# Encoder layer on one core: thirteen more wait instructions in each gate tile of TensorE's program

## The chip, the cores and the metric

The kernel runs on one core of a Trainium2 chip. The metric is the device time of one execution in microseconds; lower is better.

## What is computed

One layer of a bidirectional encoder on a sequence of 256 tokens with 2048 channels, in float32. Cut to what matters:

```python
xn = _rmsnorm(x, norm_pre_w[l])
h = xn @ w_in[l]                       # 256 x 2048 times 2048 x 13312
na_q, na_k, na_v, na_z, hg_q, hg_ff, hg_fb, hg_i, hg_z, gate_pre = jnp.split(h, splits, axis=-1)
o_a = neighbourhood_attention(na_q, na_k, na_v, na_rel_bias[l]) * silu(na_z)      # 16 heads of 64
o_b = rmsnorm(hgrn2_bidirectional(hg_q, hg_ff, hg_fb, hg_i, lb)) * silu(hg_z)     # 8 heads of 128
g = jax.nn.sigmoid(gate_pre + b_gate[l]); g_a, g_b = jnp.split(g, 2, axis=-1)     # gate_pre: 256 x 4096
y = g_a * (o_a @ w_branch[l, :NA_WIDTH]) + g_b * (o_b @ w_branch[l, NA_WIDTH:])
x = x + _rmsnorm(y @ w_out[l], norm_post_w[l])
```

## The kernel before, in words

It is written instruction by instruction: each engine has its own program, and semaphores join them. Nearly all of TensorE's work is matrix products in split precision. SyncE loads a weight tile of 1 MB into one of four `raw` buffers; ScalarE rounds each half of it into `w_hi` (L522, counted by `hi_ready`); VectorE makes the remainder `w_lo` (L762, counted by `lo_ready`); TensorE multiplies hi with hi, hi with lo and lo with hi, and tells with `half_used` that a half is free.

TensorE's program is straight code, with every loop written out when it is built. Its parts are:

- 16 early tiles (L1303) for the values of both branches;
- 8 groups of 10 tiles, one group per head pair and head (`group`, L1430). Slots 0, 1, 3, 4, 5, 7 and 9 are channel tiles (`project`, L1213): 16 products of 512 columns with `w_hi` (L1222), then 16 of 256 columns with `w_lo` (L1229). Slots 2, 6 and 8 are gate tiles (`gate_tile`, L1254, through `token_tile`, L1233): 16 products of 512 columns with `w_hi`, then 8 with `w_lo`, all on L1237;
- a tail of 8 gate tiles;
- 16 tiles of the branch projection (`token_tile` again, from `branch_tile`), and 16 tiles of the output projection (L1497 to L1499).

Between the `w_hi` and the `w_lo` products of a tile, `visits` (L1415) puts in TensorE's small work for attention and recurrence. Most of it stands in slot 3, after the 16 long products of that channel tile:

```python
if s == 3:
    if g > 0:
        heads_out(g - 1)       # 8 products, L1348
        near_session(g - 1)    # 64 products, L1370 and L1362
    if g < NG:
        both_scores(g)         # 16 products, L1335
    if g > 0:
        far_scores(g - 1)      # 2 products, L1390
```

These 90 products are in float32, each done by the engine as two matmuls, so 180 matmuls with their 180 weight loads. They are called the burst here. The burst of group g belongs to `visits(g, 3)`; the tail has one too, without `both_scores`. Slots 5 or 6 and 7 or 8 hold 4 and 2 small products more.

The first product of a channel tile waits for `hi_ready` and for `tile_out`, so one of these two stands alone; the first product of a gate tile waits for `hi_ready` only, but for the first gate tile of a block of four.

Of the kernel before, what the change touches and what calls it, by code (L numbers as in the profile page):

```python
# [47 lines left out]
IN_SLOTS = 10  # L48
I_SLOTS = (30, 31)
TAIL = 8  # L50
PRE_BLOCKS = 4
N_PRE = 4 * PRE_BLOCKS
M_IN = NG * IN_SLOTS + TAIL
N_IN = N_PRE + M_IN
# [50 lines left out]
def encoder_layer(nc, x_head, x_turned, x_rows, vectors, w_in, band_bias, b_gate, w_branch, w_out, norm_post_w, out):  # L105
# [4 lines left out]
    with ExitStack() as ctx:  # L110
        def sb(name, shape, dt=F32):
            return ctx.enter_context(nc.sbuf_tensor(name, shape, dt))

        def sem(name):
            return ctx.enter_context(nc.semaphore(name))

        act_hl = sb("act_hl", [P, KT, 2 * T], F32R)
# [3 lines left out]
        w_hi = sb("w_hi", [P, HALVES, 1024], F32R)  # L122
# [56 lines left out]
        def gate_sums(b):  # L179
            return bank[0:2] if b == GATE_BLOCKS - 1 else bank[2:4]  # L180
# [30 lines left out]
        hi_ready = sem("hi_ready")  # L211
# [46 lines left out]
        def wait(engine, semaphore, value):  # L258

            if isinstance(value, int) and value <= 0:  # L260
                return
            engine.wait_ge(semaphore, value)
# [13 lines left out]
        def gate_tile_of(g, s):  # L276

            return divmod(g * len(GATE_SLOTS) + (s if g == NG else GATE_SLOTS.index(s)), 4)
# [6 lines left out]
        def raw_count(n4, r):  # L285

            return n4 * 16 + (16 if r > 1 else 0)

        def place(g, s):

            n = g * IN_SLOTS + (N_PRE + s)
            return n, n % RAW, raw_count(n // RAW, n % RAW)
# [61 lines left out]
        def _(sp):  # L354
# [12 lines left out]
            def time_order(g):  # L367

                if g == 0:
                    sp.wait_ge(block_taken, 2 * PRE_BLOCKS)  # L370
                wait(sp, hg_out, g - 1)
# [7 lines left out]
            def load_gates(g, s):  # L379

                n, r, _ = place(g, s)
                b, part_k = gate_tile_of(g, s)
                col = GATE_TILE * P + 512 * b
                load(r, w_in_v[:, 4 * part_k:4 * part_k + 4, col:col + 512], n)

            def group(g):
                for s in range(IN_SLOTS):
                    if s == 1:
                        load_bias(g)
                    if s == 4:  # L390
                        time_order(g)
                    n, r, _ = place(g, s)
                    if s in GATE_SLOTS:
                        load_gates(g, s)
                    else:
                        col = g + COL_TILE[s]
                        load(r, w_in_v[:, :, col * P:col * P + P], n)
# [34 lines left out]
            for g in range(NG):  # L432
                group(g)
            for t in range(TAIL):
                load_gates(NG, t)
# [78 lines left out]
        def _(act):  # L514
# [10 lines left out]
            def split_tile(n, r, landed):  # L525
                split_hi(n, r, landed, 0)
                split_hi(n, r, landed, 1)
# [83 lines left out]
            def group(g, first):  # L611
                for s in range(IN_SLOTS):
                    split_tile(*place(g, s + 1))
                    if first and s == 0:
                        take_block(PRE_BLOCKS - 1)
                    if not first:
                        previous(g, s)
                    attention(g, s)
                    if s in CHANNEL_SLOTS:
                        take_part(place(g, s)[0], turn(g, s) % 2)  # L620
# [22 lines left out]
            def take_block(c):  # L643

                act.wait_ge(half_used, 8 * (c + 1))
                if c == 0:
                    act.wait_ge(rstd_ready, 1)
                for t in range(2):
                    src = bank[4 + 2 * (c % 2) + t].rearrange("p (g c) -> p g c", g=4)
                    nc.scalar.activation(token_tiles(c // 2, c % 2, t), src, ACT.Copy,  # L650
                                         scale=rstd[:, t:t + 1]).then_inc(block_taken, 1)
# [33 lines left out]
            for g in range(NG):  # L685
                group(g, g == 0)
            for t in range(TAIL):
                split_tile(*place(NG, t + 1))
# [65 lines left out]
        def _(dve):  # L754
# [10 lines left out]
            def split_tile(n, r):  # L765
                split_lo(n, r, 0)
                split_lo(n, r, 1)
# [241 lines left out]
            def group(g, first):  # L1009
                for s in range(IN_SLOTS):  # L1010
                    split_tile(*place(g, s + 1)[0:2])
                    if not first:
                        previous(g, s)
                    attention(g, s, first)
                    if s == 6 and not first:
                        mean_square(g - 1)
                    if s in GATE_SLOTS:
                        take_gates(g, s)
                    else:
                        take_tile(g, s, tile_dst[s])  # L1020
# [76 lines left out]
            for g in range(NG):  # L1097
                group(g, g == 0)
            for t in range(TAIL):
                split_tile(*place(NG, t + 1)[0:2])  # L1100
# [111 lines left out]
        def _(pe):  # L1212
# [17 lines left out]
                                               stop=(k == KT - 1), skip_group_check=True)  # L1230
                    ins.then_inc(half_used, 1)

            def token_tile(n, operand, sums, part_k, begin, end, between):  # L1233

                def product(t, h, kk, lo, weights, start=False, stop=False):
                    k, w = 4 * part_k + 2 * h + kk, slice(kk * 512, (kk + 1) * 512)
                    return nc.tensor.matmul(sums[t][:, :], operand[:, k, lo * T + t * P:lo * T + (t + 1) * P],  # L1237
                                            weights[:, (2 * n + h) % HALVES, w], start=start, stop=stop)

                for h in range(2):  # L1240
                    pe.wait_ge(hi_ready, n * 2 + h + 1)
                    for t in range(2):
                        for kk in range(2):
                            product(t, h, kk, 0, w_hi, start=(begin and h == 0 and kk == 0))
                            product(t, h, kk, 1, w_hi)
                between()
                for h in range(2):
                    pe.wait_ge(lo_ready, n * 2 + h + 1)
                    for t in range(2):
                        for kk in range(2):  # L1250
                            ins = product(t, h, kk, 0, w_lo, stop=(end and h == 1 and kk == 1))
                    ins.then_inc(half_used, 1)

            def gate_tile(g, s, between):  # L1254

                b, part_k = gate_tile_of(g, s)
                if part_k == 0 and b == GATE_BLOCKS - 1:
                    pe.wait_ge(tile_out, NG * len(CHANNEL_SLOTS))
                elif part_k == 0:
                    wait(pe, gate_out, 2 * b)  # L1260
                token_tile(place(g, s)[0], act_hl, gate_sums(b), part_k, part_k == 0, part_k == 3, between)

            def warm(count):
                for _ in range(count):
# [58 lines left out]
            def both_scores(g):  # L1323
# [3 lines left out]
                if g == 0:  # L1327
                    pe.wait_ge(band_clear, 3)
                    pe.wait_ge(block_taken, 2 * PRE_BLOCKS)
                for u in range(2):  # L1330
# [8 lines left out]
            def heads_out(g):  # L1339
                pe.wait_ge(prob_ready, g + 1)  # L1340
                v_now = big[:, 2 * g, :]
                if g == 0:
                    pe.wait_ge(block_taken, 2 * PRE_BLOCKS)
                wait(pe, oa_ready, g)
# [70 lines left out]
            def visits(g, s):  # L1415

                if s == 3:
                    if g > 0:
                        heads_out(g - 1)
                        near_session(g - 1)  # L1420
                    if g < NG:
                        both_scores(g)
                    if g > 0:
                        far_scores(g - 1)
                if g > 0 and s == (5 if g == NG else 6):
                    hgrn_sum(g - 1)
                if g > 0 and s == (7 if g == NG else 8):
                    turn_out(g - 1)

            def group(g):  # L1430
                for s in range(IN_SLOTS):
                    if s in GATE_SLOTS:
                        gate_tile(g, s, lambda: visits(g, s))
                    else:
                        n, r, _ = place(g, s)
                        wait(pe, tile_out, turn(g, s) - 1)
                        project(n, r, ps_proj[turn(g, s) % 2], lambda: visits(g, s))
# [11 lines left out]
            for g in range(NG):  # L1449
                group(g)  # L1450
            for t in range(TAIL):
                gate_tile(NG, t, lambda: visits(NG, t))
# [118 lines left out]
```

## Time and profile before

| | |
|---|---|
| Median of 3 runs | 812.17 us (812.1 to 812.62) |
| Profiled execution | 813.33 us |
| Its span, first to last instruction | 811.5 us |
| Mean granted clock of TensorE | 0.992 |
| TensorE busy | 794.9 us, 98% |
| VectorE busy | 600.9 us, 74% |
| ScalarE busy | 367.7 us, 45% |
| Moved by DMA | 159.73 MB, mean 197 GB/s |

All figures below the first line are of one profiled execution, which took 1.16 us longer than the median of the runs. Busy is the share of the span in which an engine executes; waits, branches and the issue of DMAs are not counted. Times in a window or a timeline are microseconds from the start of the span. PE is TensorE's matmuls and PEld its weight loads, which run beside them.

### The profile page before, as it was taken

What the parts mean: (1) busy time and instruction counts of PE and PEld (TensorE: products, weight loads), DVE (VectorE), ACT (ScalarE), POOL (GpSimd) and SP (SyncE); (2) the same over time, 40 slices, a digit from 0 to 9 for tenths busy, and PEclk for the clock granted to TensorE, in tenths of its full rate; (3) what the DMA queues carried; (4) which work ended last, traced back from release to release, by engine and by line L of the source; (5) the groups of instructions that cost most, each with busy time, mean ns of one, the idle gap of its engine ahead of it and who ended that gap; (6) DMA issues with size and microseconds to landing.
All of it is one profiled execution on the core that took longest, in us unless ns stands there. A gap on an engine that the chain in (4) does not pass through costs nothing.

```text
span 811.5 us, 12933 instructions
## 1 busy us (share of the span) xinstructions
PE 794.9 (98%) x5284; PEld 675.9 (83%) x5284; DVE 600.9 (74%) x1022; ACT 367.7 (45%) x578; POOL 32.2 (4%) x45
## 2 busy tenths in 40 slices
PE   9999999999989989999999999999999999999996
PEld 7888888888868878888888888888888888888885
DVE  7687559779859878888888889879884566664553
ACT  7665444444425434435335445444534434344442
POOL 4000000000000000100000000001000000000002
PEclk9999999999989999999999999999999999999999
DMA  9976387748745765775676666765647655476522
GB/s 323 395 240 196 107 261 223 191 150 226 200 134 166 200 196 146 208 208 154 189 217 168 176 194 166 191 206 174 217 157 233 238 177 202 165 264 238 175 97 104
DMA packets 167851, 159.73 MB, mean 197 GB/s; under 512 B 4208, under 2 KB 122224, under 8 KB 167152
## 3 DMA queue, kind: packets, MB, share of 16 engines
q1 hardware_dynamic: 164624, 151.03, 59.8%
q10 hardware_dynamic: 3168, 7.87, 3.6%
q8 instruction: 42, 0.69, 0.3%
q14 instruction: 17, 0.14, 0.0%
HBM read 155.74 MB, written 2.10 MB: 195 GB/s over the span
## 4 chain that ended last, share of the span: by engine, by line
PE 98%; issue 1%; DVE 0%; POOL 0%; ACT 0%; DVEq 0%; POOLq 0%
PE psum L1237 32%; PE psum L1222 25%; PE psum L1229 14%; PE psum L1303 9%; PE psum L1498 4%; PE psum L1497 4%; PE psum L1499 4%; PE psum L1273 1%; PE psum L1401 1%; PE psum L1370 1%; PE psum L1390 1%; PE psum L1348 1%; PE psum L1335 1%; PE psum L1265 0%; PE psum L1461 0%
## 5 line engine op out<-in xcount | busy, mean ns | idle before, releaser
L762 DVE TENSOR_TENSOR w_lo<-raw,w_hi 128x1024 fp32r<-128x1024 f32 x268 | 317.6, 1221 | 95.7 <-ACT w_hi L522 95.6
L522 ACT ACTIVATE w_hi<-raw 128x1024 fp32r<-128x1024 f32 x268 | 270.9, 1053 | 174.6 <-PE psum L1237 113.2
L1222 PE MATMUL psum<-act_hl,w_hi 128*128 128x512 f32 x896 | 214.1, 391 | 0.6 <-issue 0.6
L1222 PEld LDWEIGHTS psum<-act_hl,w_hi 128*128 128x128 f32 x896 | 167.1, 189 | 34.3 <-issue 0.8
L1229 PE MATMUL psum<-act_hl,w_lo 128*128 128x256 f32 x896 | 119.6, 287 | 3.1 <-issue 3.1
L1229 PEld LDWEIGHTS psum<-act_hl,w_lo 128*128 128x128 f32 x896 | 116.7, 195 | 7.0 <-issue 3.2
L1237 PE MATMUL psum<-w_hi,act_hl 128*128 128x512 f32 x512 | 122.0, 390 | 0.0
L1237 PEld LDWEIGHTS psum<-w_hi,act_hl 128*128 128x128 f32 x512 | 94.5, 188 | 18.6
L536 ACT ACTIVATE part<-psum 128x256 f32<-128x256 f32 x56 | 21.4, 382 | 151.7 <-PE psum L1229 151.7
L1237 PE MATMUL psum<-w_lo,act_hl 128*128 128x512 f32 x256 | 65.2, 396 | 0.0
L1237 PE MATMUL psum<-w_hi,branch_hl 128*128 128x512 f32 x256 | 60.6, 389 | 0.0
L1237 PEld LDWEIGHTS psum<-w_hi,branch_hl 128*128 128x128 f32 x256 | 48.1, 188 | 10.0
L1303 PE MATMUL psum<-w_hi,branch_hl 128*128 128x512 f32 x224 | 55.4, 389 | 0.0
L1237 PEld LDWEIGHTS psum<-w_lo,act_hl 128*128 128x128 f32 x256 | 46.8, 188 | 9.1
L1497 PE MATMUL psum<-w_hi,act_hl 128*128 128x512 f32 x128 | 49.9, 390 | 0.0
L1499 PE MATMUL psum<-w_hi,act_hl 128*128 128x512 f32 x128 | 49.8, 389 | 0.0
L1498 PE MATMUL psum<-w_lo,act_hl 128*128 128x512 f32 x128 | 49.8, 389 | 0.0
L1303 PEld LDWEIGHTS psum<-w_hi,branch_hl 128*128 128x128 f32 x224 | 42.0, 188 | 8.7
L779 DVE TENSOR_TENSOR hg<-psum,part 128x256 f32<-128x256 f32 x32 | 18.2, 569 | 33.3 <-ACT part L536 33.3
L561 ACT ACTIVATE prob<-prob,small 128x96 f32<-128x96 f32 x32 | 11.6, 364 | 52.6 <-DVE small L797 52.6
L1237 PE MATMUL psum<-w_lo,branch_hl 128*128 128x512 f32 x128 | 31.9, 391 | 0.0
L1303 PE MATMUL psum<-w_lo,branch_hl 128*128 128x512 f32 x112 | 29.9, 389 | 0.0
(134 smaller groups left out, 654.9 us busy)
## 6 DMA issues: line engine op xcount, KB each, us to landing
raw<-in_w_in SPq DMA_DIRECT2D x100, 1024.0 KB, 5.6
raw<-in_w_branch SPq DMA_DIRECT2D x16, 1024.0 KB, 5.1
raw<-in_w_out SPq DMA_DIRECT2D x16, 1024.0 KB, 5.0
big<-in_b_gate ACTq DMA_DIRECT2D x16, 256.0 KB, 4.4
raw<-in_w_in SPq DMA_DIRECT2D x8, 256.0 KB, 6.3
raw<-in_w_in SPq DMA_DIRECT2D x4, 512.0 KB, 9.0
big<-in_x_rows SPq DMA_DIRECT2D x2, 1024.0 KB, 14.8
big<-in_x_rows ACTq DMA_DIRECT2D x2, 1024.0 KB, 4.9
```

Source lines behind the costliest of these rows:

```text
L522: nc.scalar.activation(w_hi[:, (2 * r + h) % HALVES, :], raw[:, r, 1024 * h:1024 * (h + 1)], ACT.Copy).then_inc(hi_ready, 1)
L536: nc.scalar.activation(part[:, b, :], ps_proj[b][:, T:2 * T], ACT.Copy).then_inc(part_ready, 1)
L561: nc.scalar.activation(v, v, ACT.Exp, bias=nmax[:, i:i + 1], accum_out=rsum[:, i:i + 1]).then_inc(exp_ready, 1)
L762: nc.vector.tensor_tensor(w_lo[:, i, :], raw[:, r, 1024 * h:1024 * (h + 1)], w_hi[:, i, :].bitcast(F32), ALU.subtract).then_inc(lo_ready, 1)
L779: nc.vector.tensor_tensor(dst, src, prt, ALU.add).then_inc(tile_out, 1)
L1222: nc.tensor.matmul(sums[:, :], w_hi[:, i, w], act_hl[:, k, :], start=(k == 0), stop=False, skip_group_check=True)
L1229: ins = nc.tensor.matmul(sums[:, 0:T], w_lo[:, i, w], act_hl[:, k, 0:T], start=False, stop=(k == KT - 1), skip_group_check=True)
L1237: return nc.tensor.matmul(sums[t][:, :], operand[:, k, lo * T + t * P:lo * T + (t + 1) * P], weights[:, (2 * n + h) % HALVES, w], start=st ...
L1303: return nc.tensor.matmul(bank[4 + 2 * (c % 2) + t], x_hl[:, k, lo * T + t * P:lo * T + (t + 1) * P], weights[:, i, w], start=start, stop= ...
L1497: nc.tensor.matmul(o, hi, w_hi[:, i, w], start=(k == 0), stop=False)
L1498: nc.tensor.matmul(o, hi, w_lo[:, i, w], start=False, stop=False)
L1499: ins = nc.tensor.matmul(o, lo, w_hi[:, i, w], start=False, stop=(k == KT - 1))
```

## The change

In the gate tiles alone, two more waits for `hi_ready` stand ahead of the 2nd to the 14th of the 16 products with `w_hi`. They wait for the same value as the wait that stands ahead of that half's first product. One of the two is carried by the product, the other is an instruction of its own. The branch projection calls `token_tile` without the new argument and stays as it is. The order of the products and their operands are the same.

```diff
+GATE_FILL = 13
...
-            def token_tile(n, operand, sums, part_k, begin, end, between):
+            def token_tile(n, operand, sums, part_k, begin, end, between, fill=0):
...
                     pe.wait_ge(hi_ready, n * 2 + h + 1)
                     for t in range(2):
                         for kk in range(2):
-                            product(t, h, kk, 0, w_hi, start=(begin and h == 0 and kk == 0))
-                            product(t, h, kk, 1, w_hi)
+                            for lo in range(2):
+                                if 0 < 8 * h + 4 * t + 2 * kk + lo <= fill:
+                                    for _ in range(2):
+                                        pe.wait_ge(hi_ready, n * 2 + h + 1)
+                                product(t, h, kk, lo, w_hi, start=(begin and h == 0 and kk == 0 and lo == 0))
...
-                token_tile(place(g, s)[0], act_hl, gate_sums(b), part_k, part_k == 0, part_k == 3, between)
+                token_tile(place(g, s)[0], act_hl, gate_sums(b), part_k, part_k == 0, part_k == 3, between, GATE_FILL)
```

Nothing changes its order, but from the first gate tile on everything in TensorE's program stands at a later place. In TensorE's program before, slot 2 of group 1 (a gate tile) and slot 3 up to the small products read so; a name in brackets is what a product waits for, and "x7" are seven equal ones:

```order
L1237 MATMUL psum<-w_hi,act_hl 128x512 [waits hi_ready]
L1237 MATMUL psum<-w_hi,act_hl 128x512 x7
L1237 MATMUL psum<-w_hi,act_hl 128x512 [waits hi_ready]
L1237 MATMUL psum<-w_hi,act_hl 128x512 x7
L1237 MATMUL psum<-w_lo,act_hl 128x512 [waits lo_ready]
L1237 MATMUL psum<-w_lo,act_hl 128x512 x3
L1237 MATMUL psum<-w_lo,act_hl 128x512 [waits lo_ready]
L1237 MATMUL psum<-w_lo,act_hl 128x512 x3
L1222 MATMUL psum<-act_hl,w_hi 128x512 [waits hi_ready,tile_out]
L1222 MATMUL psum<-act_hl,w_hi 128x512 x7
L1222 MATMUL psum<-act_hl,w_hi 128x512 [waits hi_ready]
L1222 MATMUL psum<-act_hl,w_hi 128x512 x7
```

The same place in the changed program, whose lines have numbers higher by one to four:

```order
L1238 MATMUL psum<-w_hi,act_hl 128x512 [waits hi_ready] x14
L1238 MATMUL psum<-w_hi,act_hl 128x512 x2
L1238 MATMUL psum<-w_lo,act_hl 128x512 [waits lo_ready]
L1238 MATMUL psum<-w_lo,act_hl 128x512 x3
L1238 MATMUL psum<-w_lo,act_hl 128x512 [waits lo_ready]
L1238 MATMUL psum<-w_lo,act_hl 128x512 x3
L1223 MATMUL psum<-act_hl,w_hi 128x512 [waits hi_ready,tile_out]
L1223 MATMUL psum<-act_hl,w_hi 128x512 x7
L1223 MATMUL psum<-act_hl,w_hi 128x512 [waits hi_ready]
L1223 MATMUL psum<-act_hl,w_hi 128x512 x7
```

Fourteen of the gate tile's first sixteen products wait now, where two did. The channel tile behind it is as it was.

The small products that follow, in the changed program (all but the line numbers is as before):

```order
L1352 MATMUL psum<-prob_t,big 32x160 [waits block_taken,prob_ready]
L1352 MATMUL psum<-prob_t,big 32x160 x7
L1374 MATMUL psum<-hg 32x32 [waits dec_ready]
L1374 MATMUL psum<-hg 32x32 x7
L1374 MATMUL psum<-q_dec,k_dec 32x32 x24
L1374 MATMUL psum<-wide 32x32 x16
L1366 MATMUL psum<-wide 32x32 x8
L1366 MATMUL psum<-wide 32x64 x8
L1339 MATMUL psum<-k_wide,na 32x96 [waits s_taken,tile_out]
L1339 MATMUL psum<-k_wide,na 32x96 x15
L1394 MATMUL psum<-hg 128x128 [waits dec_ready]
L1394 MATMUL psum<-hg 128x128
```

Counted with the weight loads, the second matmuls of float32 products and the waits that stand alone, the burst is 361 instructions long in both programs. It begins at instruction 1700 of TensorE's program in group 1 before, and at 1752 in the changed one; from one group to the next it moves on by 985 (983 from group 1 to 2, 984 from group 4 to 5) before, and by 1024 (1022, 1023) in the changed one. The whole program has 10727 instructions before and 11143 in the changed one.

## Rows read from the trace of the kernel before

**Rows 1.** The page: TensorE's busy time, and DMA queue 8 (packets, MB, share).

```profile
PE 794.9 (98%) x5284; PEld 675.9 (83%) x5284; DVE 600.9 (74%) x1022; ACT 367.7 (45%) x578; POOL 32.2 (4%) x45
...
q8 instruction: 42, 0.69, 0.3%
```

**Rows 2.** Waits of the PE engine over the whole span: total us, times, longest us.

```profile
PE psum L1335 <- issue: 3.7, 1, 3.7
PE psum L1229 <- issue: 3.1, 1, 3.1
PE psum L1362 <- issue: 1.2, 1, 1.2
...
PE psum L1222 <- issue: 0.6, 1, 0.6
```

**Rows 3.** Timeline of PE, groups 1 to 4: start, length, instruction, idle before it.

```profile
172.84 0.24 PE L1362 MATMUL psum<-wide 128*32 128x64 f32 x1 [1.19 <-issue]
...
236.80 0.57 PE L1335 MATMUL psum<-k_wide,na 64*32 64x96 f32 x14 [3.75 <-issue]
...
302.85 2.88 PE L1229 MATMUL psum<-act_hl,w_lo 128*128 128x256 f32 x15 [3.07 <-issue]
...
367.34 0.85 PE L1222 MATMUL psum<-act_hl,w_hi 128*128 128x512 f32 x3 [0.56 <-issue]
```

**Rows 4.** Windows from burst to burst: us, busy of each engine, PEclk, DMA share, GB/s.

```profile
169.70:230.64 60.94, 59.75 (x487) 51.62 (x487) 51.05 (x98) 27.54 (x49) 2.13 (x2) 1.00 0.68 189
230.64:296.55 65.91, 62.16 (x487) 53.79 (x486) 51.27 (x99) 27.65 (x49) 1.21 (x2) 0.95 0.61 173
296.55:360.83 64.28, 61.21 (x488) 52.95 (x487) 51.41 (x99) 27.66 (x49) 3.25 (x2) 0.97 0.62 178
360.83:421.09 60.26, 59.70 (x487) 51.52 (x486) 50.78 (x99) 26.50 (x47) 2.12 (x2) 1.00 0.66 189
...
480.61:540.13 59.52, 59.52 (x487) 51.53 (x486) 51.27 (x99) 27.53 (x49) 1.21 (x2) 1.00 0.68 191
```

**Rows 5.** Windows: from stall to stall, and the first part of group 1's burst.

```profile
172.84:236.80 63.96, 60.21 (x506) 51.94 (x506) 50.08 (x97) 27.54 (x49) 2.13 (x2) 0.99 0.67 192
...
169.70:171.50 1.80, 1.80 (x144) 1.77 (x143) 0.97 (x1) 0.00 (x0) 0.00 (x0) 1.00 0.48 114
```

**Rows 6.** From 172.8 to 236.79: TensorE's separate waits by line (ns), DMA queue 8.

```profile
L1219 PEldq EVENT_SEMAPHORE  x7: 51/51/51, 173.9 to 223.0; - x7
...
L262 PEldq EVENT_SEMAPHORE  x4: 51/51/51, 172.9 to 232.3; - x4
...
L1241 PEldq EVENT_SEMAPHORE  x1: 51/51/51, 184.8 to 184.8; - x1
...
q8 instruction: 4, 0.07, 0.4%
```

**Rows 7.** Windows: the same sixteen w_lo products in group 2 and in group 5.

```profile
238.17:241.73 3.56, 3.56 (x19) 3.56 (x18) 2.00 (x7) 1.54 (x8) 0.00 (x0) 0.50 0.02 5
...
423.95:425.95 2.00, 2.00 (x20) 2.00 (x18) 1.93 (x7) 1.11 (x7) 0.00 (x0) 1.00 1.04 403
```

**Rows 8.** DMA queue 8, transfers begun in 234.3 to 234.5, 364.7 to 364.8, 538.3 to 538.4.

```profile
q8 instruction: 1, 0.02, 30.1%
...
q8 instruction: 1, 0.02, 60.1%
...
q8 instruction: 1, 0.02, 60.5%
```

**Rows 9.** A separate wait of slot 3 in group 1, and the products behind it.

```profile
L1219 PEldq EVENT_SEMAPHORE  x1: 51/51/51, 162.1 to 162.1; - x1
...
165.98 3.79 PE L1222 MATMUL psum<-act_hl,w_hi 128*128 128x512 f32 x16
```

**Rows 10.** Output projection, 720 to 790: window, and separate waits of L1508.

```profile
720.00:790.00 70.00, 70.00 (x314) 58.04 (x313) 37.39 (x37) 31.04 (x40) 0.00 (x0) 1.00 0.55 195
...
L1508 PEldq EVENT_SEMAPHORE  x26: 51/51/51, 722.1 to 789.4; - x26
```

## The prediction

> **What bounds the kernel now.** I read the page first. TensorE is busy 98% of the span [rows 1], so the time is the sum of what TensorE executes and of what keeps it from executing. The view of TensorE's waits comes next: it has no wait for a load, a weight split or a sum after the start, only four idle times put down to "issue", that is, to nothing that the profile shows: 3.7, 3.1, 1.2 and 0.6 us, 8.6 us together [rows 2]. The timeline says where: at 172.84, 236.80, 302.85 and 367.34 us, each inside or just behind the burst of small products in slot 3 of groups 1 to 4 [rows 3]. Groups 5 to 7 have the same burst and no such idle time.
>
> What is special about these places shows when one counts instructions. A product is two instructions in TensorE's program (weight load and matmul), an fp32 product that is no transpose four, and a wait that doesn't fit on a product is one more. From the end of the first stall to the end of the second there are 506 matmuls, 506 weight loads [rows 5] and 7 + 4 + 1 separate waits [rows 6]: 1024. The second to the third and the third to the fourth count 1024 too, within one or two. In such a stretch DMA queue 8 carries 4 transfers and 0.07 MB [rows 6], that is 16 KB each, and 42 of them, 0.69 MB, over the span [rows 1]; 16 KB for 256 instructions is 64 bytes each, and 42 x 256 = 10752 is the length of TensorE's program (I count 10727). So TensorE's program arrives in blocks of 256 instructions, and all four stalls stand at a block's edge. In groups 2 and 4 TensorE goes on some 2.5 us after a transfer of queue 8 begins (234.3 to 234.5, then 236.80; 364.7 to 364.8, then 367.34) [rows 3, 8]. My reading: crossing an edge asks for the block after the next, and that takes several us. A block of long products lasts about 28 us, so nobody notices; but the burst's 361 instructions take 2.9 us, and if it holds one edge and the next follows soon, the second comes before its block.
>
> The Trainium skill (Runtime: NRT & Kernel Launch, section Instruction fetch mechanics) says that engines fetch in 16 KiB blocks of 256 instructions and that crossing a boundary is mostly hidden. The trace agrees with the size; by "mostly hidden" the change would bring nothing, and that is the third rival below.
>
> **What the stalls cost, the clock included.** From burst to burst a group takes 60.94, 65.91, 64.28 and 60.26 us for groups 1 to 4, and 59.52 where there is no stall [rows 4]. The excess is 1.42 + 6.39 + 4.76 + 0.74 = 13.31 us. It is more than the 8.6 us of idle time, because behind the two long stalls the granted clock is 0.5 (1.2 GHz), after 3.75 and 3.07 us in which TensorE did nothing [rows 3]. Sixteen products of 256 columns take 3.56 us there and 2.00 us in group 5, at 2.4 GHz [rows 7].
>
> **Where the change puts the edges.** It adds 13 separate instructions to each gate tile (of its two waits one rides on the product). A group with three gate tiles goes from 985 to 1024 = 4 x 256. Before, the edges wander: counted from the start of the burst, the first edge in or next to it stands at 30 in group 1, 70, 109, 148, 188 and 227 in groups 2 to 6, at 10 in group 7 and 84 in the tail. The next one is 256 later; the first is the one that asks, the next the one that needs. Stalls came at 286, 326, 365 and 404; at 444 and 483 the burst is over by 81 and 120 instructions and long products have given the fetch its time. After the change the phase no longer moves. Up to the burst of group 1, four gate tiles have put in 52 instructions, so the asking edge stands 22 before the burst and the needing one at 234, in groups 1 to 7 alike (24 before and 232 in the tail, within one or two).
>
> The nearest case is group 7 before: asking edge at 10, transfer begun at 538.3 to 538.4, 1.8 us before the burst at 540.13 [rows 8], and no stall, though the needed edge stands in mid burst. The sequencer runs ahead: a separate wait at 162.1 belongs to a tile whose first product starts at 165.98 [rows 9], 3.9 us ahead. That tile's 16 long products are over when the burst starts at 169.70 [rows 4]: 0.23 us each. In the new program the asking edge stands 32 instructions earlier than in group 7, all among long products: 16 products at 2 instructions each, or 11 at 3, at 0.23 us 2.5 to 3.7 us. The transfer would begin some 4.3 to 5.5 us ahead of the burst, and the block be there 2.5 us later, before the burst begins. It is needed about 1.6 us into it (144 products in the first 1.80 us of group 1's [rows 5]). That leaves 3.4 to 4.5 us, and a fetch that starts 3 us late still does no harm. The third edge stands at 490, behind 16 short and some 50 long products. **So all four stalls and both spells of low clock go: -13.3 us.** What is late next: nothing near. Groups 5 to 7 run at 59.52 us with TensorE busy throughout, over the same loads and splits.
>
> **What the waits cost.** 32 gate tiles (24 in groups, 8 in the tail) get 13 each: 416 separate waits, and as many that ride. Each is for a value of hi_ready that the tile's first wait of that half has already seen, so none ever waits for ScalarE. A separate wait takes TensorE's sequencer 51 ns [rows 6]. From below the cost is 0: from 720 to 790 us 26 separate waits stand between long products and TensorE is busy for 70.00 of 70.00 us [rows 10], since the sequencer is ahead. From above it is 416 x 0.051 = 21.2 us, if none is covered. I take 0. A long product takes 230 ns; the burst shows that the sequencer can hand over 361 instructions in 2.9 us, 8 ns each, so one wait and two instructions need some 70 ns of every 230. Nothing is queued behind a wait but these products. A riding wait costs nothing that I can see: the products that carry one now, the first of each half, stand in the same busy stretch. Below 0 there is a few tenths at most, if the fetch for other blocks shifts. The two more blocks to fetch (44 for 42) are 32 KB beside 160 MB. SyncE, VectorE and ScalarE get the same instructions in the same order.
>
> **Sum.** The profiled execution took 813.33 us (span 811.5): 813.3 - 13.3 + 0 = 800.0. The median of the runs is 1.2 us below the profiled execution, so 812.2 - 13.3 = **798.9 us**.
>
> **Rivals.**
> (a) *The waits are not covered.* With one before every product the sequencer might lose its lead, or a wait might hold back the weight load behind it, which now runs beside the product before. The point from which this decides is a wait that costs over 230 - 16 = 214 ns of the sequencer, or one that breaks the overlap. At 51 ns exposed each: 798.9 + 21.2 = 820.1, slower. For it: no row has 13 such waits in a row. Against: 51 ns is far below 214, and the waits in rows 10 cost nothing. 6%.
> (b) *The fixed phase is a bad one.* If I misplaced the edge or the lead, all bursts stall alike: eight times the 4.76 of group 3 would be 38, so 798.9 + 38 = 837; eight times the 1.42 of group 1, 810. For it: all four stalls are 4 blocks apart, and the new program puts each such fourth edge at 234 of a burst. Against: group 7 had its needing edge at 266 with a later asking edge, and didn't stall. 5%.
> (c) *Nothing changes*, because the stalls are no fetches, or because fetches are hidden as the page above has it: 812. Against: the count of 1024 and rows 8. 4%.
> (d) *A part is given back*: one or two bursts still wait a little, when a transfer on queue 8 comes late behind the 1 MB loads, or a few ns of each wait show: 2 to 6 us, 801 to 805. 9%.
> The forecast itself: 76%.
>
> **How the numbers follow.** 0.2% is 1.6 us, about what a measurement of this kernel can tell from no change. Faster: the forecast and (d), and the mild end of (b): 0.86. Same: (c), 0.04. Slower: (a) and the rest of (b), 0.10. The range goes from 797.0 (the forecast with 1.9 us for blocks fetched better elsewhere and for the difference between profiled and other executions) to 804.5, most of (d); that leaves out (a), (b), (c), some 15 to 20%.
>
> **What the profile after would show.** Right: no "issue" idle over 0.3 us behind a burst; burst to burst 59.5 us in groups 1 to 6; clock 1.0 through the middle; 44 transfers on queue 8, each one per burst beginning 4 us before it; long products in gate tiles still 0.23 us apart, with separate waits of 51 ns between. The prediction would be wrong with 8 like gaps at 234 instructions into each burst (b), with gate products further apart (a), or with the gaps of rows 2 in the same places (c).

## The result, and the profile after

The changed kernel takes 799.89 us (median of 4 runs, 799.42 to 799.95), the kernel before 812.23 us: a ratio of 0.9846, 95% interval 0.9829 to 0.9863. It is 12.3 us faster; the forecast was 798.9 us, in a range of 797.0 to 804.5.

From the page of the changed kernel: span, TensorE's busy time, its granted clock in 40 slices, and DMA queue 8.

```profile
span 797.7 us, 13349 instructions
...
PE 789.4 (99%) x5284; PEld 671.3 (84%) x5284; DVE 600.8 (75%) x1022; ACT 367.6 (46%) x578; POOL 32.3 (4%) x45
...
PEclk9999999999999999999999999999999999999998
...
q8 instruction: 43, 0.70, 0.3%
```

The same 5284 matmuls are busy for 5.5 us less than in [rows 1]: that is mostly the low clock, gone from the middle of the span (groups 1 to 4 of [rows 4] were busy for 4.7 us more than four times 59.52). TensorE's waits are these two and no more; what [rows 2] put down to "issue" has no counterpart:

```profile
PE psum L1269 <- POOL small L458: 1.1, 1, 1.1
PE psum L1277 <- ACT branch_hl L634: 0.2, 1, 0.2
```

The windows from burst to burst in groups 1 to 3 answer to [rows 4] (columns as there); groups 4 to 6 read 59.51, 59.53 and 59.52:

```profile
169.24:228.75 59.51, 59.51 (x487) 51.51 (x486) 51.02 (x98) 27.54 (x49) 3.27 (x2) 1.00 0.68 194
228.75:288.28 59.53, 59.53 (x488) 51.52 (x487) 51.26 (x99) 27.52 (x49) 1.21 (x2) 1.00 0.67 191
288.28:347.80 59.52, 59.52 (x488) 51.53 (x487) 51.38 (x99) 27.55 (x49) 2.12 (x2) 1.00 0.68 192
```

Queue 8 begins a transfer in 222.7 to 222.9, one in 283.6 to 283.7 and one in 401.3 to 401.5, which answers to [rows 8]:

```profile
q8 instruction: 1, 0.02, 31.4%
q8 instruction: 1, 0.02, 64.5%
q8 instruction: 1, 0.02, 33.4%
```

The bursts of these groups begin at 228.75, 288.28 and 407.31, that is 6.0, 4.6 and 5.9 us later. In groups 1 to 7 it is 4.6 to 6.0 us, and 3.8 us in the tail. And the 416 added waits are there, 51 ns each, on the line of the change:

```profile
L1248 PEldq EVENT_SEMAPHORE  x416: 51/51/51, 102.0 to 606.1; - x139
```

### The profile page after: what moved, and what is told of

Same layout as the page of the kernel before. It is cut to its first block, busy times and chain, and to the rows that moved or that the text cites. A ratio compares the mean times of both kernels' runs of the same rounds, so it can differ in the third digit from the quotient of the medians.

```text
span 797.7 us, 13349 instructions
## 1 busy us (share of the span) xinstructions
PE 789.4 (99%) x5284; PEld 671.3 (84%) x5284; DVE 600.8 (75%) x1022; ACT 367.6 (46%) x578; POOL 32.3 (4%) x45
## 4 chain that ended last, share of the span: by engine, by line
PE 98%; DMA 0%; DVE 0%; ACT 0%; DVEq 0%; POOL 0%; issue 0%
PE psum L1238 33%; PE psum L1223 26%; PE psum L1230 13%; PE psum L1307 10%; PE psum L1501 4%; PE psum L1503 4%; PE psum L1502 4%; PE psum L1277 1%; PE psum L1405 1%; PE psum L1374 1%; PE psum L1352 1%; PE psum L1394 1%; PE psum L1339 0%; PE psum L1465 0%; DMA na<-in_x_head 0%; PE psum L1366 0%
## 5 line engine op out<-in xcount | busy, mean ns | idle before, releaser
L1230 PEld LDWEIGHTS psum<-act_hl,w_lo 128*128 128x128 f32 x896 | 114.3, 191 | 3.9
L1230 PE MATMUL psum<-act_hl,w_lo 128*128 128x256 f32 x896 | 116.9, 284 | 0.0
```

Of the source, the lines that this page charges most:

```text
L1230: ins = nc.tensor.matmul(sums[:, 0:T], w_lo[:, i, w], act_hl[:, k, 0:T], start=False, stop=(k == KT - 1), skip_group_check=True)
```

## The experiments

The theory: a block edge of TensorE's program inside or just ahead of the burst asks for a block, and 256 instructions on it is needed; the place of the edges alone decides. "Edge at 72" means that the asking edge stands 72 instructions after the burst's start. The positions below are counted in the built programs.

### e1: the riding waits alone

```diff
-                                if 0 < 8 * h + 4 * t + 2 * kk + lo <= fill:
-                                    for _ in range(2):
+                                if 0 < 8 * h + 4 * t + 2 * kk + lo <= fill and 4 * t + 2 * kk + lo > 0:
+                                    for _ in range(1):
```

> One wait more, not two, ahead of 12 of the gate tile's products: each rides on its product, and no instruction is added (program 10727 long, as before). Theory (block edges): the edges stand where they stood, so the four stalls are back at 1.4, 3.9, 3.4 and 1.0 us and the time is that of the kernel before, 812.2, within 0.5. Rival (the waits themselves help, by pacing TensorE or holding back weight loads): much of the 12.3 us gain stays, about 800 to 806.

Measured: 812.93 us (10 runs) beside 812.35, ratio 1.0003 (0.9993 to 1.0013). The stalls are back. TensorE's waits:

```profile
PE psum L1339 <- issue: 3.7, 1, 3.7
PE psum L1230 <- issue: 2.9, 1, 2.9
PE psum L1366 <- issue: 1.4, 1, 1.4
...
PE psum L1223 <- issue: 0.3, 1, 0.3
```

So it isn't the waiting that helps, but the 39 places that the other waits of a group take. In this execution groups 1 to 4 took 61.12, 65.13, 64.15 and 59.98 us, 12.3 us over four times 59.52, where the one of [rows 4] had 13.3: the stalls are not of one size.

### e2: the same length, by waits in other tiles

```diff
+                        if 0 < k <= fill:
+                            for _ in range(2):
+                                pe.wait_ge(hi_ready, n * 2 + h + 1)
                         nc.tensor.matmul(sums[:, :], w_hi[:, i, w], act_hl[:, k, :], ...
...
+                                13 if s in (NSLOT_Q, NSLOT_B, NSLOT_HZ) else 0)
```

> The 39 separate waits of a group stand in three channel tiles (slots 0, 4 and 9), 13 in each, and none in the gate tiles; groups are 1024 long and the asking edge stands 20 before each burst, as in the changed kernel. The tail has no added wait, so its edge stands at 28, where group 1 of the kernel before had it (30) and lost 1.4 us. Theory: groups 1 to 6 at 59.5 us as in the changed kernel, one stall of 1 to 2 us in the tail, 800.5 to 802. Rival (it matters that the waits stand in gate tiles): stalls in groups 1 to 4 stay, about 812.

Measured: 799.67 us, ratio 0.9841 (0.9825 to 0.9856). Groups 1 and 2, and the tail's burst:

```profile
169.05:228.57 59.52, 59.52 (x487) 51.55 (x487) 51.07 (x98) 27.54 (x49) 3.26 (x2) 1.00 0.67 193
228.57:288.09 59.52, 59.52 (x487) 51.56 (x487) 51.26 (x99) 27.54 (x49) 1.21 (x2) 1.00 0.70 192
...
585.44:588.25 2.81, 2.64 (x149) 2.37 (x149) 0.42 (x1) 0.00 (x0) 0.00 (x0) 1.00 0.78 275
```

In gate tiles or in channel tiles, the instructions do the same; what counts is how many stand ahead of the burst. The expectation of the tail missed, and with it that of the time, 800.5 to 802: the tail's burst took 2.81 us, and 2.36 to 2.37 where it isn't disturbed, so the edge at 28 cost 0.4 us there and not 1 to 2. The transfer that it asked for began at 585.0, 0.4 us before the burst; in group 1 of the kernel before it began at 170.3, 0.6 us behind the burst's start. Why the tail asks earlier was not tested.

### e3: groups of 1024 with the edge in the wrong place

Added to the changed kernel, in its early tiles, once, for 164 separate waits in all, two waits ahead of products 3 to 8 of each half:

```diff
+                                if 4 * t + 2 * kk + lo > 1 and padded[0] < EARLY_PAD:
+                                    padded[0] += 1
+                                    for _ in range(2):
+                                        pe.wait_ge(hi_ready, n * 2 + h + 1)
```

> The changed kernel with 164 separate waits more, once, spread over the early tiles: groups stay 1024 long, but the asking edge stands at 72 of each burst (group 2 of the kernel before had it at 70 and lost 6.39 us, the low clock included). Theory: every one of the seven groups loses about 6.4 us, the tail (68) 0 to 1: 799.9 + 45 = 845, between 838 and 850, with idle of 3.5 to 4 us in each burst and the granted clock at 0.5 behind each. Rival (only each fourth block is late, those at which all four stalls of before stood): here the needed edges are of another set of four, no stalls, 800. Rival (1024 as such is good): 800.

Measured: 833.4 us (one run). Every burst stalls, 22.0 us of idle in seven groups (and 0.8 us at the same place of the tail, which the view puts down to ScalarE), and four of the windows from burst to burst, groups 1, 2, 3 and 5, read:

```profile
PE psum L1346 <- issue: 22.0, 7, 4.5
...
169.43:230.05 60.62, 59.86 (x488) 51.65 (x487) 51.06 (x98) 27.54 (x49) 2.13 (x2) 1.00 0.66 190
230.05:295.16 65.11, 61.20 (x487) 52.89 (x487) 51.27 (x99) 27.65 (x49) 1.21 (x2) 0.97 0.62 175
295.16:362.02 66.86, 62.40 (x487) 53.97 (x487) 51.42 (x99) 27.66 (x49) 2.12 (x2) 0.95 0.59 171
...
427.31:488.42 61.11, 59.85 (x487) 51.68 (x487) 50.69 (x98) 27.53 (x49) 3.25 (x2) 1.00 0.62 178
```

Length 1024 as such is worth nothing: this kernel has it and is 33.5 us slower than the changed one, with 164 covered waits more. "Each fourth block" falls too. But the sum expected was 845: five groups lost 5.6 to 7.3 us, groups 1 and 5 only 1.1 and 1.6. With the edge in one place the stall still had two sizes, so the place of the edges does not decide alone.

### e4: groups of 985, all edges moved by 120

The same addition of e3 with 120 separate waits, in the kernel before.

> The kernel before with 120 separate waits once, spread over the early tiles; groups 985 long. Edges in bursts of groups 1 to 7 and the tail: 166, 206, -10, 28, 68, 108, 146, 220 (negative: ahead of the burst). Theory: groups 1 to 3 and the tail without stall; groups 4, 5, 6, 7 lose what 1, 2, 3, 4 lost, 1.4, 6.4, 4.8 and 0.7 us; total 812 to 813. Rival (the stalls belong to groups 1 to 4, by their gate bias loads or other transfers): the stalls stay at groups 1 to 4 and none comes in 5 to 7.

Measured: 809.08 us (one run). Groups 1, 3, 4, 5 and 6, from burst to burst (group 2 is like 1; group 7 took 60.08 for 59.27):

```profile
169.82:229.34 59.52, 59.52 (x488) 51.56 (x487) 51.05 (x98) 27.54 (x49) 3.27 (x2) 1.00 0.67 194
288.86:348.38 59.52, 59.52 (x488) 51.55 (x487) 51.40 (x99) 27.54 (x49) 3.25 (x2) 1.00 0.67 191
348.38:409.11 60.73, 59.80 (x487) 51.67 (x487) 50.78 (x99) 26.50 (x47) 2.11 (x2) 1.00 0.66 188
409.11:470.80 61.69, 59.78 (x488) 51.68 (x487) 50.71 (x98) 27.53 (x49) 3.25 (x2) 1.00 0.61 177
470.80:535.16 64.36, 61.23 (x487) 52.94 (x486) 51.28 (x99) 27.64 (x49) 1.21 (x2) 0.97 0.63 178
```

The four stalls went from groups 1 to 4 to groups 4 to 7, as the theory said and the rival excluded. They cost 1.2, 2.2, 4.8 and 0.8 us, 9.0 in all: the second one is 4.2 us cheaper than in the kernel before, and that is the 3 to 4 us that the total fell short of 812 to 813. Experiment e5 tells why.

### e5: what makes a stall long

One difference stood out between e3's cheap and dear groups: when SyncE issued the load for slot 8. In the five dear groups it was issued 0.55 us before the burst, in the cheap groups 1 and 5 it came 1.0 and 0.65 us behind the burst's start. (e4's cheap group 5 had it 0.64 us behind, its dear group 6 0.55 us before.) The lines show group 2 of e3: the issue, TensorE going on, and the DMA view from 232.2 to 236.2 (each digit is 0.1 us), which shows what the transfer of queue 8 does:

```profile
229.50 0.37 SPq L362 DMA_DIRECT2D raw<-in_w_in  x1
...
236.37 0.57 PE L1346 MATMUL psum<-k_wide,na 64*32 64x96 f32 x13 [3.91 <-issue]
...
DMA  9999999999999995416000000000000000000000
...
q1 hardware_dynamic: 333, 0.65, 41.8%
q8 instruction: 1, 0.02, 1.6%
```

It begins at 234.0 (a window of 234.0 to 234.2 holds it alone with one last packet of the load), at the moment the load's packets run out. Nothing is moved behind it, and TensorE goes on at 236.37. The edit, in SyncE's program:

```diff
+                    if s == NSLOT_G2 and g > 0:
+                        sp.wait_ge(s_done, g + 1)
```

> The kernel of e3 (edge at 72 of every burst), with one wait more on SyncE: the 1 MB load for slot 8 is held until the burst's 16 score products are done. In e3 the transfer on queue 8 began within 0.3 us of the moment at which that load's packets ended, 3 to 4 us after the edge; in groups 1 and 5, where the load was issued 0.65 to 1.0 us after the burst's start instead of 0.55 before it, it began 0.3 to 0.5 us after the edge, and the group lost 1.1 and 1.6 us instead of 5.6 to 7.3. Theory (the program's transfer waits behind the load's packets): all seven groups lose 1.0 to 1.7 us, no low clock, 808 to 812 in all. Rival (the delay is the fetch's own, or hangs on something else): 833 as in e3.

Measured: 812.47 us (8 runs), 20.9 less than e3, with the edge in the same place. Group 2 again: when the load of slot 8 is issued, when TensorE goes on, and the DMA view from 231.0 to 235.0:

```profile
234.73 0.37 SPq L362 DMA_DIRECT2D raw<-in_w_in  x1
...
234.27 0.39 PE L1348 MATMUL psum<-k_wide,na 64*32 64x96 f32 x13 [0.98 <-issue]
...
DMA  4321000000500000000000000000000000000000
```

The transfer begins at 232.0, not 234.0, and the group takes 60.85 us, not 65.11:

```profile
230.87:291.72 60.85, 59.87 (x488) 51.68 (x487) 51.23 (x99) 27.54 (x49) 1.21 (x2) 1.00 0.67 187
...
353.02:416.08 63.06, 61.40 (x488) 53.08 (x487) 50.80 (x99) 26.61 (x47) 3.25 (x2) 0.97 0.62 181
```

Six groups lost 1.3 to 1.8 us; group 4 lost 3.5, since the clock fell there once more, which the expectation had excluded. The sum of the seven is 13.1 us in the profiled execution, which took 814.14 us and was one of the dearer; the median is half a microsecond over the expected 808 to 812. So the load ahead of it delays the program's transfer: that is the long part of a long stall. The 2.2 us from its start to TensorE's next product stay in any case.

Not every load in flight holds the transfer back until its packets end. In group 1 of the changed kernel the same load is in flight when a transfer begins at 172.9, and its packets run on at the full rate behind it (window 172.8 to 174.2):

```profile
q1 hardware_dynamic: 264, 0.54, 100.3%
q8 instruction: 1, 0.02, 4.3%
```

The transfer of [rows 8] at 538.3 and one of e6 at 227.3 begin amid a load too, one whose packets have 512 bytes where those of slot 8 have 2 KB. What in the load decides was not tested.

### e6: how far the edge may move

Five waits for thirteen in the first four gate tiles, so that the edge stands at 12 of all bursts:

```diff
-                token_tile(place(g, s)[0], act_hl, gate_sums(b), part_k, part_k == 0, part_k == 3, between, GATE_FILL)
+                token_tile(place(g, s)[0], act_hl, gate_sums(b), part_k, part_k == 0, part_k == 3, between,
+                           5 if g == 0 or (g, s) == (1, NSLOT_G0) else GATE_FILL)
```

> The changed kernel with 32 of the first 52 separate waits taken out (5, not 13, in the gate tiles of group 0 and the first of group 1): groups from 1 on stay 1024 long, the asking edge stands at 12 of each burst, where group 7 of the kernel before had it (10) without a stall. Theory: no stall or a few tenths in some groups, 799.5 to 801.5. Rival (an edge inside a burst always costs): 1 to 6 us per group, 807 to 840.

Measured: 799.85 us, ratio 0.9854 (0.9837 to 0.987), no wait of TensorE but the one at the start, and groups 1 to 6 at 59.52 us each. In group 2 the transfer begins in 227.3 to 227.4, 1.7 us before the burst at 229.05. (In group 1 the edge stands at 10, as the burst begins 32 instructions earlier than in the changed kernel.) So 12 is still safe, 28 cost 0.4 and 1.2 us (e2, e4), 30 cost 1.4 to 1.6, 70 and more up to 7.3.

### e7 and e8: what a separate wait costs

Last four tiles of the tail, ahead of 20 of each 24 products; e8 has 16 for the 8. `MANY` counts calls of `wait_ge`, and eight of them make four separate instructions: one wait rides on the product, and in these builds a separate instruction holds up to two. (So not every further wait becomes an instruction of its own, as the description of the kernel before has it.)

```diff
+MANY = 8
...
+                                if 4 * t + 2 * kk + lo > 0 and fill == MANY:
+                                    for _ in range(fill):
+                                        pe.wait_ge(hi_ready, n * 2 + h + 1)
...
+                            if 2 * t + kk > 0 and fill == MANY:
+                                for _ in range(fill):
+                                    pe.wait_ge(lo_ready, n * 2 + h + 1)
```

> The changed kernel with 4 separate waits (not 1) ahead of each of 20 of the 24 products of the last four tail tiles: 272 separate waits more, all seen before. Price by its length, 51 ns: 4 x 51 + 16 = 220 ns per product, less than the 227 of a product. Theory: covered, 799.9 and the tail tiles 5.5 us each. Rival (each wait costs TensorE something): 272 x 51 ns = 13.9 us, 813.8.

> As e7 with 8 separate waits ahead of each of the 20 products: 592 more than the changed kernel. The sequencer needs 20 x (8 x 51 + 16) + 4 x 16 = 8.5 us per tile of 5.5, so it falls behind: 4 x 3.1 = 12.2 us, less the 4 us that it is ahead at the start: 8 to 9 us, 808 to 809, with 0.42 us from product to product at the end. Rival (a satisfied wait is as cheap to the sequencer as a matmul, 8 ns, and 51 ns is only how it is recorded): 800.

Measured: 812.13 us (8 runs) with four, 847.36 us (2 runs) with eight. Both expectations fail, and both on the same number. That e7's rival had 813.8 is luck: it takes each of 272 waits for 51 ns, but they cost 45 ns each here and the 592 of e8 cost 80 ns each. In e8, eight separate waits ahead of one product (window 595.06 to 595.85):

```profile
L1249 PEldq EVENT_SEMAPHORE  x8: 51/51/51, 595.1 to 595.8; - x8
```

Seven steps in 0.7 us: each is recorded with 51 ns, but the next one starts some 106 ns later. In the trace the starts lie 105 or 106 ns apart, whether the instruction holds one wait or two. The changed kernel shows the rest of the price: 261 of its 416 separate waits start 125 or 126 ns after the one before, with a product's weight load and matmul between, which leaves 20 ns for these two. A product with four costs the sequencer 4 x 106 + 20 = 444 ns, nearly twice the 227 that TensorE needs for it. Three tail tiles of the changed kernel (from the first product of tile 4 to that of tile 7), the same of e7, and one tile of e7:

```profile
590.14:607.18 17.04, 17.04 (x81) 14.23 (x79) 9.83 (x16) 8.47 (x16) 0.68 (x1) 1.00 0.58 163
```

```profile
590.18:616.04 25.86, 25.71 (x81) 13.44 (x79) 9.94 (x17) 9.10 (x16) 0.68 (x1) 1.00 0.47 143
606.86:616.04 9.18, 9.14 (x26) 4.18 (x24) 2.37 (x3) 2.81 (x5) 0.00 (x0) 1.00 0.68 171
```

9.18 us for a tile: 20 x 0.444 is 8.9, and its last four products take little. Four tiles are 3.7 us too long each, 14.7 in all; 12.2 were measured, and the 2.5 between are, by an estimate, what the sequencer was ahead. In e8 the same sum is 20 x 0.87 = 17.4 a tile, 12 too many, 48 for four. Measured are 47.5, some 2 us more than this less the lead; what they are is open. The granted clock was 0.50 from 597.0 to 620.8 and from 627.7 to 658.3, but a price for that was not separated.

### e9: the kernel before, with the load held

The edit of e5 in the kernel before.

> The kernel before (985 long, edges in its bursts at 30, 70, 109, 148 of groups 1 to 4), with SyncE's 1 MB load for slot 8 held until the burst's score products are done, as in e5. The block edges stay. Theory (edge and load together): group 1 as before (1.4 us; its load came after the edge already), group 2 1.3 to 1.9 instead of 6.4, group 3 1 to 1.7 instead of 4.8, group 4 nothing instead of 0.7, no low clock or one short spell: 812.2 - 13.3 + 4.4 = 803.3, between 802 and 805. Rival (the load only happened to end there): 812.

Measured: 804.38 us, ratio 0.991 (0.9893 to 0.9926). Groups 1 to 4:

```profile
169.82:230.69 60.87, 59.75 (x487) 51.62 (x487) 51.05 (x98) 27.54 (x49) 2.13 (x2) 1.00 0.66 189
230.69:292.11 61.42, 59.87 (x487) 51.65 (x487) 51.27 (x99) 27.54 (x49) 1.21 (x2) 1.00 0.66 186
292.11:352.76 60.65, 59.68 (x487) 51.59 (x486) 51.39 (x99) 27.66 (x49) 3.25 (x2) 1.00 0.64 189
352.76:412.28 59.52, 59.52 (x487) 51.52 (x486) 50.79 (x99) 26.49 (x47) 2.12 (x2) 1.00 0.65 192
```

1.4 + 1.9 + 1.1 + 0 = 4.4 us over, as expected, with no low clock. One wait on SyncE wins more than half of what the change wins, and no instruction of TensorE moves. In the changed kernel, e2 and e6 TensorE has at most 0.2 us of "issue" idle left that it could gain; the two changes together were not run. No version tried beats the changed kernel by more than the runs scatter: 799.89, 799.67 and 799.85 are one time.

## Why the prediction was right

- **What the stalls are.** Right, by e1 to e4 together: the same length without the place (e3), the place without the length (e4), the length by other instructions (e2), the waits without the length (e1). In e3 and e4 every "issue" stall stood within three instructions of the forecast edge, counted by the trace's records. That 42 x 256 gave the program's length was chance, though: there is one transfer for each edge, and edges stand at 1730, as in group 1, and at each 256 instructions before and behind it.
- **What they cost.** The step took 13.31 us from one execution and set it against the median of the runs. The medians differ by 12.3, the two profiled executions by 13.9 (813.33 and 799.42). The stalls vary, as e1's 12.3 us in four groups shows, and the profiled execution of before was among the dearer ones: its mean granted clock was 0.992, and of the runs of this kernel beside the experiments ten with that clock took 812.1 to 814.1 us, 25 with 0.994 or 0.995 took 811.0 to 812.5. So the size of this term was a microsecond too large for the median, and 798.9 that much too low: the sum should have scaled the stalls with the execution.
- **Clock.** Right: 16 products took 3.56 us for 2.00 in the kernel before, and after the change the clock stays at 2.4 GHz from burst to burst.
- **Where the edges go.** Right. The transfer was to begin 4.3 to 5.5 us ahead of the burst and begins 4.6 to 6.0 ahead. I named 44 transfers on queue 8; there are 43, as many as edges in 11143 instructions (42 in 10727). The count of 81 and 120 instructions behind the burst should be 83 and 122 for edges needed at 444 and 483; nothing hangs on it.
- **How the asked block comes.** "Takes several us" hid two things. Some 2.2 to 2.8 us pass from the transfer's start to the next product, and before that a load can hold it up, as e5 and e9 show. I named a transfer that comes late behind the 1 MB loads only as rival (d); with the low clock that follows it is the larger part of what groups 2 and 3 lost: 6.4 and 4.8 us, and 1.9 and 1.1 in e9 with the load held.
- **What the waits cost.** 0, right, but by a wrong sum, and so in part by luck: the true price is nearly double and still fits. I took 51 + 16, some 70 ns, of the sequencer's time per product; it is 106 + 20 = 126 of 227. The step that failed is the price of a separate wait taken from its recorded length [rows 6]. Rows 10 couldn't show it, since 26 waits in 70 us are covered at any such price. One wait a product is covered; two would need 2 x 106 + 20 = 232 ns by this estimate, which no run tried, and four lost 12 us.
- **Rivals.** (a) is refuted at one wait a product and true at four. (b) didn't happen, but e3 is such a case, with the edge elsewhere: 833.4 us, where I had put 837. That they are close is luck, since e3's seven stalls cost 1.1 to 7.3 us and not 4.8 each. (c) is refuted. The Trainium skill (Runtime: NRT & Kernel Launch, section Instruction fetch mechanics) calls the crossing of a 16 KiB boundary mostly hidden. The changed kernel agrees (43 transfers, no stall); e3 doesn't, where one boundary in a burst cost 1.1 to 7.3 us. The Trainium skill (Advanced Engine Details and Errata, section ISA Cache) speaks of 256 instructions to a line and of two lines only, though it also gives 128 KB for TensorE, which would be eight lines of 16 KB. The runs fit two: after an edge one whole block is at hand, and the stall comes 256 instructions on (e3 to e5).

## What to carry to other kernels

When an engine that should be bound by its own work shows "issue" gaps, count its instructions between them, waits and weight loads too: gaps at multiples of 256, as here, point to the program arriving late, and moving the edges by a few added waits tests it (e4). Where a few hundred instructions run in a few us, see that only one block edge falls in them and that the one before comes several us earlier, and try holding a large load back until the fetch is through (e5, e9); check the place of the edges after each edit that changes the count. Take an instruction's price from the distance between starts in a row of them, not from its recorded length.

## What the runs showed of the hardware that was not expected

- TensorE's program comes in blocks of 256 instructions (16 KB, one transfer on queue 8 for each edge), and a load of 1 MB can hold such a transfer back: it began at 234.0 with the load and at 232.0 without it, at the same edge (e3, e5). It isn't so for every load: at 172.9 in the changed kernel and at 227.3 in e6 a transfer began amid one.
- A separate wait that is already satisfied occupies TensorE's sequencer for 106 ns and is recorded with 51. Waits that ride on products cost nothing that e1 shows (812.93 beside 812.35 us, with 12 of them in each gate tile).
- The sequencer hands over weight loads and matmuls at 8 ns each in the burst (361 in 2.86 us), so a separate wait takes the time of some 13 of them.
- The granted clock was 1.2 GHz for 3.4 or 6.8 us in or just behind every idle time over 3 us (before, e1, e3, e4), and behind one of 1.66 us in group 4 of e5, but not behind one of 1.91 us in group 5 of e4 or of 1.55 us in e9. In e8 it fell at 597.0, after 4.7 us in which TensorE was busy for 2.66 us and never idle for more than 0.5 us at a time. So the length of one idle time doesn't decide it.
